# The order of the next pair's latent query pieces in a four-branch attention trunk

## What is computed

```
q = (rms_norm(c_q) @ w_uq)            # per head: 64 plain columns, 32 that get a rotary turn
q = concat(q[:64], rope(q[64:]))
k = concat(k_plain, rope(k_rope))     # one turned key part for all heads
softmax(q k^T / sqrt(96)) @ v
```

## Time and profile before

| what | value |
| --- | --- |
| timed runs, median (lowest to highest) | 3325.31 us (3321.79 to 3330.41) |
| the profiled execution, its own time | 3328.77 us |
| span of that execution | 3326.8 us |
| TensorE busy (matmul) | 3079.5 us, 93% |
| VectorE busy | 1690.5 us, 51% |
| ScalarE busy | 1021.2 us, 31% |
| GpSimd busy | 551.1 us, 17% |
| mean granted TensorE clock | 0.978 of full |

### The profile page before, as it was taken

One profiled execution on the slowest core, in us unless ns is written; L12 is line 12 of the kernel. 1 busy time (PEld: TensorE's weight loads), 2 busy tenths in 40 slices (PEclk: granted clock), 3 DMA queues, 4 the chain that ended last, 5 costly groups with the idle time before them and its releaser, 6 DMA issues. The chain is left out here.

```text
span 3326.8 us, 39909 instructions
## 1 busy us (share of the span) xinstructions
PE 3079.5 (93%) x14214; PEld 1750.7 (53%) x14214; DVE 1690.5 (51%) x4511; ACT 1021.2 (31%) x2757; POOL 551.1 (17%) x994
## 2 busy tenths in 40 slices
PE   4989999999898999989998999999998989999998
PEld 3435666655455565544443456665554555555443
DVE  4224887776666534422121258877766664344222
ACT  1223343333344333310002333333343433333000
POOL 0000222121111123310000012221111111333000
PEclk8999999999999999999999999999998999999999
DMA  6000110111000012042210001111110000210321
GB/s 217 28 20 32 39 45 30 32 36 46 15 20 15 13 31 97 15 150 66 61 60 21 27 32 41 39 30 39 34 50 14 15 14 20 79 50 21 109 78 58
DMA packets 91003, 153.04 MB, mean 46 GB/s; under 512 B 12656, under 2 KB 68224, under 8 KB 88504
## 3 DMA queue, kind: packets, MB, share of 16 engines
q1 hardware_dynamic: 90808, 150.50, 13.9%
HBM read 120.36 MB, written 32.21 MB: 46 GB/s over the span
## 5 line engine op out<-in xcount | busy, mean ns | idle before, releaser
L940 PE MATMUL ps_s<-xT,w_ring 128*128 128x348 f32 (+2 forms) x3616 | 1139.5, 469 | 5.1 <-DVE gate L1303 2.4
L940 PEld LDWEIGHTS ps_s<-xT,w_ring 128*128 128x128 f32 x3616 | 677.0, 192 | 399.3 <-issue 104.5
L1461 POOL TENSOR_SCALAR arena<-arena,small 128x256 f32<-128x256 f32 (+9 forms) x576 | 363.3, 643 | 1610.3 <-DVE small L1378 1609.0
L1152 ACT ACTIVATE arena<-arena,small 128x256 f32<-128x256 f32 (+9 forms) x576 | 380.3, 660 | 199.3 <-DVE small L1366 198.9
L1163 ACT ACTIVATE arena<-ps_t 128x512 f32<-128x512 f32 (+4 forms) x700 | 309.3, 472 | 372.1 <-PE ps_t L1007 363.5
L1007 PE MATMUL ps_t<-ident,arena 128*128 128x128 f32 (+2 forms) x2432 | 356.5, 274 | 50.3 <-ACT arena L1163 34.6
L1197 DVE MAX8 small<-score 128x8 f32<-128x1040 f32 (+6 forms) x448 | 376.2, 840 | 10.5
L1199 DVE MATCH_REPLACE8 score<-small,score 128x1040 f32<-128x1040 f32 (+6 forms) x448 | 369.8, 825 | 0.0
L1007 PEld LDWEIGHTS ps_t<-ident,arena 128*128 128x128 f32 (+2 forms) x2432 | 253.4, 131 | 209.4 <-issue 97.7
L984 PE MATMUL ps_s<-feat 64*128 64x256 f32 (+12 forms) x1888 | 310.2, 430 | 29.2 <-DVE small L1366 24.4
L1019 PE MATMUL ps_o<-arena 128*64 128x256 f32 (+3 forms) x2816 | 312.3, 358 | 20.7 <-ACT cT L1086 12.1
(11 more groups left out here) (125 smaller groups left out, 2330.3 us busy)
## 6 DMA issues: line engine op xcount, KB each, us to landing
w_ring<-in_w_feat SPq DMA_DIRECT2D x78, 512.0 KB, 3.5
mixed<-mixg SPq DMA_DIRECT2D x128, 128.0 KB, 1.7
feat<-mixed SPq DMA_DIRECT2D x16, 1024.0 KB, 6.7
resid<-score SPq DMA_DIRECT2D x16, 512.0 KB, 3.1
score<-resid SPq DMA_DIRECT2D x16, 512.0 KB, 7.5
arena<-in_w_out SPq DMA_DIRECT2D x4, 1536.0 KB, 8.1
cT<-falls SPq DMA_DIRECT2D x8, 520.0 KB, 4.8
feat<-falls SPq DMA_DIRECT2D x8, 520.0 KB, 5.2
```

The lines of the kernel that those rows point to most:

```text
L940: mm = pe.matmul(ps_s[:, bank, 0:w], w_ring[:, wt % 2, k, :], xT[:, k, c0:c0 + w], start=(k == 0), stop=(k == KT - 1))
L1152: nc.scalar.activation(p, p, ACT.Exp, scale=-1.0, bias=nm[:, e:e + 1], accum_out=psums[0:M, st % 4, e:e + 1]).then_inc(S["exp_done"], 1)
L1461: nc.gpsimd.tensor_scalar(p, p, rinv[0:M, st % 4, e:e + 1], 1.0, ALU.mult, ALU.mult).then_inc(S["nrm_done"], 1)
```

## The change

The six pieces keep their places (idx 3, 4, 5, 6, 7, 7 in B; 4, 5, 6, 7, 8, 8 in the last pair of D) but are taken in the order R, R, R, N, N, N where it was N, N, N, R, R, R. Nothing is added or removed.

```diff
     def q_latent(self, l, p):
         return [lambda c=c, what=what: self.add("qb", l=l, p=p, what=what, cols=CHUNKS[c],
                                                 **self.group("act" if what == "N" else "dve", P_BANK))
-                for what in "NR" for c in range(3)]
+                for what in "RN" for c in range(3)]
```

## The result

The changed kernel takes 3281.16 us (median of four runs, 3279.82 to 3281.63) against 3323.55 us for the kernel before in the same comparison (3319.92 to 3330.41): ratio 0.9863, 95% interval 0.9851 to 0.9876, a gain of 42 us. The forecast was 3290 with a range of 3276 to 3311. In a second comparison on another occasion the changed kernel took 3280.51 us and the one before 3328.32 us, ratio 0.9859 (0.9843 to 0.9875).

What follows compares the result with a forecast made beforehand. TensorE, busy in 93% of the span, was taken as the bound, so only its standstills could give time back. B's 12.7 and D's 4.7 us make 17.4 a layer, 34.8 in two, giving 3290; range 3276 to 3311.

Steps and rivals of the forecast that it cites:

- The lower end of the range, 3276: Whole kernel: better by 14 us, most of the 8.4 us a layer charged for new waits and clock.
- What a tail costs, 25.9 us a layer: Pair tails of D and B: bank 4 waits plus low clock after them, 25.9 us a layer, the most returnable.
- a sign of being wrong: Tail, idx 7: line 949 waiting for L1129 in the new trace would show the forecast wrong.
- New waits in B, 2.1, 0.7 and 0: B pairs 0, 1, 2: new waits of 2.1 (1.0 + 0.4 + 0.7), 0.7 and 0 us.
- kb sooner by 2.6, 5.6 and 5: Pairs of B: kb starts about 2.6, 5.6 and 5 us earlier, measured from the pair's start.
- D, 3.7 of new waits: End of D, idx 4 to 6: moved chains cost 4.1 us, less 0.4 saved at the tail.
- Charges for a low clock after new gaps, 0.6 in B and 1.3 in D a layer: After new waits: B's return cut from 13.3 to 12.7 us, D's from 6.0 to 4.7, for low clock.
- second rival: D, idx 4 to 6: longer gaps lower the clock for half its matmuls, 9.5 us more a layer, 3309.5; 12%.
- slower rival: B idx 3 to 5, D 4 to 6: VectorE becomes the bound, 24 chains delay TensorE in full, 3335; 5%.

Runs made afterwards that it cites:

- after_again: The changed kernel itself, unaltered, measured again beside other variants: 3280.51 us.
- after_early: Changed kernel with bank 4 released by the second instruction of the turned chain instead of the fourth: 3285.06 us.
- front_early_rates: Changed kernel with D's R pieces first in their idx, bank 4 released by the chain's second instruction, and B's top-256 steps re-spread: 3295.61 us.
- after_long: Changed kernel with the last copy of each turned chain made four times instead of once: 3302.69 us.

## Why the prediction was right

The mechanism, the place and the sign of the main steps held, and the time lies in the range, 9 us below the number given. By its own terms the forecast is 24 us of standstill returned (18.7 less 3.7 and 2.8 of new waits a layer, doubled) and 10.5 us of clock (7.15 less 1.9 of charges a layer, doubled). The two traces show 26.4 and 22.5 us. So the waits were forecast well and the clock at half its size. The lower end of the range, 3276, was argued from new waits and clock charges that might not come; most of the new waits came, and what brought the time near that end was for a good part clock that had no price. That the range held it is to this extent luck.

- *What a tail costs, 25.9 us a layer.* The waits were all found and are gone but for 0.2 and 0.53 us. The low clock inside the tail is gone too. That the two layers repeat each other holds for the waits and not for the clock: the end of D took 43.46 us in layer 0 and 44.38 in layer 1, with the same standstill of 12.86, so doubling layer 0 left out 0.9 us.
- *New waits in B, 2.1, 0.7 and 0.* Measured 1.70 (0.98 + 0.19 + 0.53), 0.23 and 0, in layer 1 1.92, 0.23 and 0. R2's 1.0 was exact in layer 0. Pair 1's 0.7 was a round guess for shorter top steps, three times too large. One of these waits, N2's 0.53 for line 1129 at idx 7, is also what the prediction named as a sign of being wrong, though it had itself put 0.7 there for pair 0; as it was worded, the sign contradicts the forecast itself.
- *kb sooner by 2.6, 5.6 and 5.* By the stretches of layer 0, with the clock of line 984 and line 940 taken out (2.0 + 1.7 in pair 0, 1.7 in pair 2), 3.3, 6.3 and 5.6.
- *D, 3.7 of new waits.* The waits of line 905 and of the pieces between them add to 6.0 us after (1.52 + 0.88 + 0.50 + 0.88 + 1.69 + 0.55) and to 2.4 before (1.17 + 0.34 + 0.19 + 0.66), 3.7 more, and N2's new wait at the tail makes it 3.9. The prediction had 4.1 less 0.4. By place it is 1.2, 1.0 and 1.4 us where 1.4 to 1.5, about 1.1 and 1.5 were put, so the sum is close and each term a little smaller; the next maxima did lie behind each chain as described.
- *Charges for a low clock after new gaps, 0.6 in B and 1.3 in D a layer.* In this trace these were not due: 840 to 885 us, all of D's end, has a granted clock of 1.00 and stood at 0.95 before. That is the step that was mis-sized, by 3.8 us. In the second trace of the changed kernel D's end has 1.00 in one layer and 0.96 in the other, where it takes 39.9 us, so there the 1.3 came once.
- *Not priced:* the first long group of the next pair, whose clock also rose, some 4 us a kernel. I had taken the 6.6 us there for the group's own time. Together with the 3.8 us above, B's smaller new waits (1.5 us in both layers) and a wait for ScalarE at idx 3 that the prediction left out (0.58 us before, 0.42 after, in six pairs, 1.0 in all), this makes some 10 us; the gain exceeded 34.8 by 8 to 13.

The granted clock in these stretches, changed kernel (columns as in the earlier trace rows):

```profile
840.00:885.00 45.00, 32.91 (x157) 15.79 (x155) 32.07 (x93) 20.38 (x61) 5.40 (x12) 1.00 0.06 21
885.00:950.00 65.00, 61.84 (x404) 37.66 (x404) 48.69 (x153) 30.64 (x76) 12.68 (x18) 1.00 0.05 17
```

Against the micro-idle rule of the Trainium skill, page "TensorE: Matmul & The Clock Gate", section "A second HAM failure mode: psum-queue depth-cycling", which was weighed as the second rival: here D's end has 12 us of standstill in 45, in pieces of up to 1.7, and this trace shows the higher clock throughout. In other traces with much the same waits the stretch took 1 to 2 us longer at times (39.9 in after_again and 40.6 in after_early, at granted clocks of 0.96 and 0.92), so the rule is not refuted as a possibility; for waits of this length its size, 9.5 us a layer in the rival, is. For waits twice as long it is not: front_early_rates, with 3.1 to 3.5 us in the same places, loses 6.8 and 8.4 us a layer in this stretch to the lower clock.

The slower rival asked that over four fifths of each moved chain show on TensorE. For the chains themselves it was far less: new waits came to some 5.6 us a layer (3.7 in D, 1.9 in B) for 12 chains of 1.97 us, a quarter. But after_long shows that it was not far: of the next 1.11 us on each chain 57% shows as standstill, and with the clock that follows it the time grows by over four fifths. With a chain of 3.1 us the changed kernel is 23 us under the kernel before, whose chain stayed at 1.97; what the old order would cost with the longer chain no run shows.

## What to carry to other kernels

A piece of filler work costs what stands in front of its last reader in that engine's queue, and the reader's own time (here 7.6 and 4.8 of the 12.4 us of waits in B a layer), not what its matmuls take: before laying one in, read the queue of the engine that frees its buffer, and put the slow reader where that queue has idle time and the fast reader where the next user of the buffer comes soon. Freeing the buffer sooner does not help when the same chain also delays the work behind it; the wait only moves one item on. And move the bulk filler (here the top-256 steps) along with it: a shift of these steps alone was worth 27 us before the change, and another one 5 us after it.

## What was not expected of the hardware

Nearly half of what the traces differ by, 22.5 of 48.9 us, is busy time of TensorE, that is clock. And the clock after a standstill is a draw with two outcomes: the same wait of 1.5 us, followed by the same 16 records, gives 4.9 or 6.6 us in one and the same execution. With the long standstills of the tail shortly before it the slow outcome was more frequent (23 of 26 against 35 of 70 over all traces); what decides it in a single case stays open. The kernel with fewer standstills is also the steadier one: eight runs of the changed kernel lie within 3.7 us, those of the kernel before reach from 3319 to 3333. The times go with the granted clock (3319 us at 0.981 or 0.982, 3330 at 0.978), but the draw above does not explain them, as it falls more evenly, and so should scatter more, in the changed kernel; where the clock differs between the runs is not shown.
